# Seventh sequence in the last stage: second half of the output weights fetched ahead of its keys, first output tile computed ahead of its scores

## The reference: what is computed

```
proj = h @ w_in                      # 1024 -> 4 * 1024
q, k, v, g = split(proj)             # 8 heads of 128; q and k normalised
s = q . k_all * scale - slope * distance      # k_all: 1024 rows of the cache, then 4 new ones
                                     # of 4 past blocks of 256 keys, the 3 with the best gate score
p = softmax(s);  o = p @ v_all
y = x + gate(c) * ((o * SiLU(g)) @ w_moba_out)   # w_moba_out: 1024 x 1024
```

## Time and profile before

| what | value |
|---|---|
| median of 3 runs | 668.54 us |
| lowest, highest | 667.92, 669.15 us |
| the profiled execution's own time | 667.59 us |
| its span | 665.8 us |
| PE busy in the span | 620.9 us (93%) |
| DVE busy | 373.3 us (56%) |
| ACT busy | 231.4 us (35%) |
| POOL busy | 223.4 us (34%) |
| transferred | 190.28 MB, 286 GB/s over the span |

### The profile page before, as it was taken

The page is one execution under the profiler, slowest core; times in us unless marked ns, Lnnn a source line. Parts: engine busy times, 40 slices in busy tenths (PEclk is TensorE's granted clock), DMA queues, the critical chain, the costliest instruction groups (busy, mean ns, idle before and its releaser), DMA issues. The chain is left out here.

```text
span 665.8 us, 11278 instructions
## 1 busy us (share of the span) xinstructions
PE 620.9 (93%) x4285; PEld 383.1 (58%) x4285; DVE 373.3 (56%) x718; ACT 231.4 (35%) x475; POOL 223.4 (34%) x239
## 2 busy tenths in 40 slices
PE   5789999999999999989999999999999998878996
PEld 4547646664666466643566756767744456443542
DVE  3333837483748374835543743335798875774723
ACT  4245232523252326214043515555134145341010
POOL 0051228022802280223176148999920012020000
PEclk9989999999999999989999999999999989797999
DMA  8997374887587748894796573344999999999993
GB/s 306 377 389 270 127 253 170 305 315 252 181 320 288 253 151 321 319 354 154 266 338 230 206 244 143 127 158 146 392 349 403 410 408 407 409 401 408 402 369 111
DMA packets 82193, 190.28 MB, mean 286 GB/s; under 512 B 4119, under 2 KB 12583, under 8 KB 82012
## 3 DMA queue, kind: packets, MB, share of 16 engines
q1 hardware_dynamic: 80484, 183.70, 74.4%
q0 software_dynamic: 1120, 4.46, 1.9%
q10 hardware_dynamic: 536, 1.41, 0.6%
HBM read 167.14 MB, written 22.41 MB: 285 GB/s over the span
## 5 line engine op out<-in xcount | busy, mean ns | idle before, releaser
L534 POOL TENSOR_TENSOR weights_low<-ring,weights_high 128x512 fp32r<-128x512 f32 x96 | 124.0, 1339 | 79.5 <-PE bank L781 43.1
L1352 ACT ACTIVATE weights_high<-ring 128x1024 fp32r<-128x1024 f32 x84 | 86.4, 1054 | 103.2 <-PE bank L800 78.6
L792 PE MATMUL bank<-weights_high,h_high 128*128 128x512 f32 x272 | 109.7, 403 | 0.0
L792 PE MATMUL bank<-weights_high,h_low 128*128 128x512 f32 x272 | 107.2, 394 | 0.0
L800 PE MATMUL bank<-weights_low,h_high 128*128 128x512 f32 x272 | 82.3, 401 | 0.9 <-DVE weights_low L534 0.9
L792 PEld LDWEIGHTS bank<-weights_high,h_high 128*128 128x128 f32 x272 | 51.4, 189 | 26.4 <-issue 15.1
L534 DVE TENSOR_TENSOR weights_low<-ring,weights_high 128x512 fp32r<-128x512 f32 x72 | 44.8, 686 | 27.8 <-PE bank L781 16.4
L800 PEld LDWEIGHTS bank<-weights_low,h_high 128*128 128x128 f32 x272 | 50.0, 188 | 14.3 <-DVE weights_low L534 3.9
L792 PEld LDWEIGHTS bank<-weights_high,h_low 128*128 128x128 f32 x272 | 51.4, 189 | 11.1
L1870 DVE TENSOR_TENSOR partial_low<-bank,partial_high 128x512 fp32r<-128x512 f32 x26 | 17.9, 688 | 67.6 <-ACT partial_high L1303 38.8
L1667 POOL TENSOR_TENSOR keys_by_sequence<-key_parts,consts 128x2048 fp32r<-128x2048 f32 x4 | 15.1, 3765 | 111.2 <-DVE key_parts L1965 111.2
(11 more groups left out here) (257 smaller groups left out, 1009.8 us busy)
## 6 DMA issues: line engine op xcount, KB each, us to landing
ring<-in_w_ada SPq DMA_DIRECT2D x12, 2048.0 KB, 12.8
ring<-in_cache_k SPq DMA_DIRECT2D x40, 512.0 KB, 10.5
ring<-in_cache_v SPq DMA_DIRECT2D x40, 512.0 KB, 9.5
ring<-in_w_ret_in SPq DMA_DIRECT2D x8, 2048.0 KB, 10.6
ring<-in_state_ret SPq DMA_DIRECT2D x32, 512.0 KB, 8.4
out_state_sample<-ring SPq DMA_DIRECT2D x32, 512.0 KB, 6.2
ring<-in_w_moba_in SPq DMA_DIRECT2D x8, 2048.0 KB, 8.7
arena<-in_cache_k SPq DMA_DIRECT2D x24, 512.0 KB, 10.4
```

The source lines that it names most:

```text
L534: tensor_tensor(w_low[:, slot, k, :], ring[:, slot, k * CH:(k + 1) * CH], high[:, k, :].bitcast(F32), ALU.subtract).then_inc(low_ready[LOW ...
L792: pe.matmul(o[i][:, :], xs[p][i][:, k, :], high[:, k, :], start=k == 0 and p == 0, stop=False)
L1352: nc.scalar.activation(w_high[u[0] == "moba"][:, 2 * i:2 * i + 2, :].rearrange("p a b -> p (a b)"), w[:, 2 * i * CH:(2 * i + 2) * CH], ACT ...
```

## The change

Two things are moved, and nothing is added or taken away. On SP, the DMA for the second half of the output weights, with its wait for the last prompt scores, goes from ahead of values 5 to ahead of keys 6. On PE, `out_tile(1, 1)` goes ahead of `sample_scores(6)`.

```
-                if (kind, a, b) == ("v", 5, 0):
+                if (kind, a, b) == ("k", 6, 0):
 
                     wait_full(sp, ("pS", MH - 1))
                     sp.dma_start(w_last, t["w_moba_out"][0].rearrange("(k p) n -> p k n", p=P)[:, :, CH:2 * CH]
...
             exps_turned(5)
+            out_tile(1, 1)
             sample_scores(6)
-            out_tile(1, 1)
             sample_values(5)
```

## The result

The changed kernel takes 670.21 us, the median of 15 runs (668.79 to 674.35). The kernel before takes 668.18 us, the median of 15. The ratio is 1.0042, with a 95% interval of 1.0023 to 1.0060: slower by 2.8 us (1.5 to 4.0); the two medians are 2.0 us apart. One run of the kernel before took 715.33 us, against at most 672.94 in the others: it counts in the median, but the ratio is taken without it. The profiled execution took 669.28 us, with a span of 667.5.

A forecast was written before the change was run, and what follows sets the result against it. Bound: saturated transfers, with the chain through the last page of keys 7, its turn and scores 7. Transfers 0, DVE +0.3, clock +1.4, less 0.2 gave +1.5 us on the median 668.54: 670.0 us, range 667.8 to 672.3.

The forecast's parts named there:

- The transfers cost nothing: On SP's queue: weights ahead of keys 6 leave the engines full, keys 7 land at 622.5 as before; cost 0.
- a shift by over 0.5 us: Sign against the forecast: keys 7 landing at another time by more than 0.5 us.
- The dry line on SP: Rival: values 5 issued too late behind keys 6, delaying keys 7; +1 to +3 us on top, 671 to 673, chance 0.08.
- The tile fills the first hole but for 4.2 us: On PE ahead of scores 6: the moved tile starts at 594.42, and 4.2 us of the hole stay open.
- A hole of 2.0 to 4.6 us ahead of scores 7: On PE: idle from 622.6 to 625.2 until keys 7 are turned at 627.2, where 0.45 stood.
- DVE late by 0 to 0.9 us, 0.3 taken: On DVE: softmax of sequence 6 and the first tile's addition delay the turn of keys 7; +0.3 us.
- The clock falls, 0 to 2.8 us, 1.4 taken: On PE behind the hole ahead of scores 7: work at the low clock adds 1.4 us; chance 0.45.
- The 0.58: PE's speed at the low clock as a share of full speed, taken from scores of 3.66 against 6.29 us.
- Less 0.2 for a wait for values 6: On PE behind scores 7: a small wait for values 6 may take up 0.2 us of the delay.
- No change: Rival: the clock holds, or falls at no cost; +0 to +0.4, 668.5 to 668.9 us, chance 0.37.
- Faster: Rival: keys 7 turned earlier through a faster line of transfers between 580 and 622 us; 664 to 668, chance 0.10.
- The fixed cost of about 2.0 us: Per DMA, set against the 5.3 us lead of values 5 on SP: by it the lead suffices and the sum stays.

The follow-up runs named there:

- half-filled kernel: The changed kernel with 7 matmuls that nobody reads ahead of the scores of sequence 7, filling half of the hole there: 0.9990 of the kernel before.
- the fifth: The kernel before with only out_tile(1, 1) moved ahead of the scores of sequence 6, the weights' DMA where it was: 1.0121 of the kernel before.
- e10: The kernel before with 22 matmuls that nobody reads in its hole ahead of the scores of sequence 6: 1.0041 of the kernel before.
- e4: The kernel before with one matmul in place of eight in the tile between scores 6 and values 5: 1.0043 of the kernel before.

## Why the prediction was right

The time forecast was 670.0 us and the measured one is 670.21, with the mechanism that was forecast. That the two times agree within 0.2 us is partly luck. The forecast added 1.5 us to a median of 668.54; the median of the 15 runs is 668.18, and the change cost 2.0 us by the medians and 2.8 by the ratio. The steps:

- *The transfers cost nothing: right.* The weights' DMA went out with the last prompt scores (577.98, and these end at 577.94), landed 11.2 us later, and the DMA share stood at 1.05 and 1.04 in the two windows about scores 7. Keys 7 landed 1.6 us earlier than forecast in the first profile after, together with all that stands ahead. The prediction named a shift by over 0.5 us as a sign against it; by its words the first profile met that sign, but it was badly chosen, since it didn't allow for where the execution stood. In the second profile after they land at 622.6, against the forecast 622.5. The dry line on SP did not come: the issues behind the weights took 6.96 us and not 11.42.
- *The tile fills the first hole but for 4.2 us: right*, 3.56 and 4.46 us in the two profiles of the changed kernel.
- *A hole of 2.0 to 4.6 us ahead of scores 7: right*, 3.44 and 2.82.
- *DVE late by 0 to 0.9 us, 0.3 taken: nearly right.* It was 0 and 0.1 in the two profiles, but 1.6 in that of the half-filled kernel, outside the bounds. There the turned keys 6 came at 607.39 and the scores took 6.48, so they ended at 613.9. The bound had used 612.8.
- *The clock falls, 0 to 2.8 us, 1.4 taken: the mechanism is shown, the size was low.* Scores 7 lost 1.5 to 1.7 us in each of the five profiles with a fall there, a little over the 1.4. The 0.58 behind that figure was misread: of the 6.29 us of scores 6, from 601.05 to 607.34, only the part up to 606.4 ran at 0.50. In the changed kernel 3.3 us at 0.50 lost 1.6, about half. What was missing is the end. With the clock down at scores 7, the first product of the sample rows was slow as well in all five profiles; with the clock up there it was slow in four of the six kernels without filling at the end. Where both happen the end comes 3.3 us later than where neither does, and 1.6 later than where only the second does. The measured loss of 2.0 to 2.8 us lies between these two. Its intervals, from 0.4 us at the lowest to 4.0 at the highest, take in the 1.6 alone as well, so that the end has a part in the loss is seen in profiles and not in the times. That the fall at scores 7 makes the one at the end more likely isn't shown: five profiles of the one kind and six of the other can't tell it.
- *Less 0.2 for a wait for values 6: not there.* PE goes from the tile to values 6 without idle time in the profile of before (637.90) and in that after (637.88), so there was nothing to take up.
- *The rivals.* "No change" is refuted by the intervals of both measurements; it was right in its condition, for holes of 1.79 us and less. "Faster" has fallen: PE was ready early, and the line of transfers had no gap to close. Nor did it run dry, with keys 7 in at 622.6. The fixed cost of about 2.0 us that the prediction took from the Trainium skill, "DMA: Bandwidth & Descriptors", section "Anatomy of one DMA — SWDGE (gpsimd) path", is told there for DMAs that GpSimd issues. Those here go out from SP, no run shows the figure, and nothing above rests on it.
- *The bound on the clock's cost.* The Trainium skill, "TensorE: Matmul & The Clock Gate", section "Part 1: The HAM clock gate (the "warmup" mystery)", puts the ramp penalty below 1% of a typical span. What this change adds, 0.42%, is below that. It is only a part of what the clock costs this kernel: with a mean granted clock of 0.971 in the profile of before and the two levels 1.00 and 0.50, it was low for about 39 of the 665.8 us, an estimate, and what that costs in all no run here shows.

That the loss is the hole ahead of scores 7, and the clock behind it, is shown from both sides. Filling the hole with useless work removes the loss (1.0006, 0.9990, 0.9994), and opening one in the kernel before, by less work (1.0043) or by faster work (1.0041), makes it, and closing that one removes it again (0.9986). How much of the loss falls on scores 7 and how much on the end stays open.

## What to carry to other kernels

Before work is moved ahead of a wait, ask what sets the pace behind it: where a saturated line of transfers delivers the next operand at a fixed time, work done earlier buys only idle time, and it is worth asking where that idle time comes to stand. Here a hole of 2.4 to 3.4 us right ahead of the critical chain was followed by half the clock at the start of that chain, in all five profiles that have one, and four of these five kernels were 2 to 3 us slower (the fifth, 8 us, lost time ahead of it too). A hole of 3.6 to 5.9 us further ahead, with slack behind it, had no cost that the runs could see. A few matmuls that nobody reads closed the hole at no cost that the runs could see, and are a quick test for it.

## What the runs showed that was not expected

- A kernel got slower by 2.7 us because a step off the chain got faster by 2.6 us (e10), and another by 2.9 us with 6.1 us less work (e4).
- The waits of 1.06 and 0.75 us near the end are enough for a fall of the clock in most profiles without filling there (nine of eleven), and then cost 1.7 us (40.3 to the end, against 38.6, where scores 7 were fast). Six unread matmuls in them kept the first product at 1.92 us in all three kernels that have them. The medians, at 0.9992, 0.9990 and 0.9994 with intervals some 0.5% wide, don't show a gain from it.
- Executions of one kernel differ more than the effect: the 35 runs of before beside the last four kernels reach from 663.59 to 672.80 us. With one or two runs of each kernel the loss could not have been told from this spread.
